# MLP products by one level of Strassen's algorithm, on one core

## The reference

```python
        x = x + merged @ w_out

        hm = _rmsnorm(x, g_mlp)
        x = x + jnp.square(jax.nn.relu(hm @ w_mlp_in)) @ w_mlp_out

    return _rmsnorm(x, g_final)
```

## Time and profile before

| | |
|---|---|
| time, median of 3 runs (lowest to highest) | 4360.57 us (4352.41 to 4361.17) |
| span of the profiled execution, first to last instruction | 4350.5 us |
| what the median has beyond that span | 10.1 us |
| TensorE busy in the span | 98% |
| the MLP stage in it | 3454.5 to 4350.5 us, 896 us |
| mean granted clock of TensorE | 0.994 |

### The profile page before, as it was taken

The page is one execution under the profiler, slowest core; times in us unless marked ns, Lnnn a source line. Parts: engine busy times, 40 slices in busy tenths (PEclk is TensorE's granted clock), DMA queues, the critical chain, the costliest instruction groups (busy, mean ns, idle before and its releaser), DMA issues. The chain is left out here.

```text
span 4350.5 us, 47027 instructions
## 1 busy us (share of the span) xinstructions
PE 4260.0 (98%) x18730; PEld 2510.2 (58%) x18730; DVE 1434.4 (33%) x3584; ACT 954.2 (22%) x1758; POOL 137.0 (3%) x215
## 2 busy tenths in 40 slices
PE   7999999999999999989999999999999999999999
PEld 4776666776556668567544565665544444444446
DVE  3246663664131255456255111112223300000003
ACT  4233332332123311154234111111111000000001
POOL 0000000000000000032010000010000000000000
PEclk9999999999999999999999999999999999999999
DMA  5310003112001111130121111122232011111111
GB/s 214 138 47 8 8 7 68 38 42 99 29 29 33 47 56 47 49 113 33 44 67 34 36 42 57 53 74 86 73 112 100 22 42 39 39 39 39 41 51 39
DMA packets 106458, 242.91 MB, mean 56 GB/s; under 512 B 15288, under 2 KB 47402, under 8 KB 105151
## 3 DMA queue, kind: packets, MB, share of 16 engines
q1 hardware_dynamic: 99264, 224.55, 16.0%
q0 software_dynamic: 5920, 13.25, 1.2%
q10 hardware_dynamic: 1056, 2.10, 0.1%
HBM read 202.80 MB, written 39.34 MB: 56 GB/s over the span
## 5 line engine op out<-in xcount | busy, mean ns | idle before, releaser
L2480 PE MATMUL upper_banks<-sbuf 128*128 128x512 f32 (+2 forms) x2112 | 812.2, 542 | 0.3 <-PEq L68 0.3
L345 PE MATMUL upper_banks<-sbuf 128*128 128x512 f32 x1792 | 769.8, 592 | 1.2 <-DVE sbuf L455 0.9
L2480 PEld LDWEIGHTS upper_banks<-sbuf 128*128 128x128 f32 x2112 | 392.7, 199 | 379.0 <-issue 373.7
L345 PEld LDWEIGHTS upper_banks<-sbuf 128*128 128x128 f32 x1792 | 340.2, 190 | 429.4 <-issue 427.1
L1894 PE MATMUL gla_prod<-sbuf 128*128 128x512 f32 (+1 forms) x784 | 319.7, 563 | 0.0
L1370 PE MATMUL mls_banks<-sbuf 128*128 128x512 f32 (+1 forms) x768 | 282.3, 522 | 2.0 <-PEq L68 1.5
L1894 PEld LDWEIGHTS gla_prod<-sbuf 128*128 128x128 f32 x784 | 147.5, 192 | 151.8 <-issue 143.8
L1370 PEld LDWEIGHTS mls_banks<-sbuf 128*128 128x128 f32 x768 | 143.1, 191 | 118.1 <-issue 110.8
L2726 ACT ACTIVATE sbuf<-upper_banks 128x512 f32<-128x512 f32 (+1 forms) x124 | 72.4, 584 | 618.3 <-PE upper_banks L2480 569.6
L860 PE MATMUL mla_banks<-sbuf 128*128 128x512 f32 (+1 forms) x416 | 176.0, 511 | 0.0
L423 ACT ACTIVATE sbuf<-upper_banks 128x1024 f32<-128x1024 f32 x32 | 32.8, 1024 | 622.5 <-PE upper_banks L345 622.5
(11 more groups left out here) (461 smaller groups left out, 5305.7 us busy)
## 6 DMA issues: line engine op xcount, KB each, us to landing
sbuf<-in_l_w_in SPq DMA_DIRECT2D x59, 512.0 KB, 3.8
sbuf<-in_w_in SPq DMA_DIRECT2D x52, 512.0 KB, 4.1
sbuf<-in_w_mlp_in SPq DMA_DIRECT2D x32, 512.0 KB, 3.6
sbuf<-in_w_mlp_out SPq DMA_DIRECT2D x32, 512.0 KB, 3.6
sbuf<-in_l_w_mod SPq DMA_DIRECT2D x24, 512.0 KB, 5.2
scratch_gates<-sbuf SPq DMA_DIRECT2D x48, 256.0 KB, 3.0
sbuf<-scratch_gates SPq DMA_DIRECT2D x8, 1536.0 KB, 6.6
sbuf<-in_l_w_mod SPq DMA_DIRECT2D x8, 1024.0 KB, 15.5
```

Source lines behind the costliest of these rows:

```text
L345: last = nc.tensor.matmul(prod[:, n % NB, o:o + 512], w[:, n % NB, k * P:(k + 1) * P], rhs, start=k == 0, stop=k == KD - 1)
L2480: last = nc.tensor.matmul(dst, lhsT, rhs, start=k == 0, stop=k == KD - 1)
```

## The change

The step pairs two output tiles, q and q+4, and takes both weight tiles at once (A, cut in 2 x 2 blocks: output tile q or q+4 by the first or last four k) against the activations (B, cut in 2 x 2: the first or last four feature rows by the first or second 512 tokens). In place of eight products of four matmuls, the step has seven, named P1 to P7, after Winograd's form of Strassen's algorithm:

- sums of weights, per step on GpSimd (line 374 on): S1 = A21 + A22, S2 = S1 - A11, S3 = A11 - A21 (in place of A21), S4 = A12 - S2, four instructions of 128 x 512;
- sums of activations on VectorE: T1 = B12 - B11, T3 = B22 - B12 (in place of B12), T2 = T3 + B11, and B21 - T2 for P4; once for `x` at the start (`xT`), once for each pair of hidden tiles (`twist_first`, `twist_last`, `hT`);
- sums of products: bank 0 of a step's three gathers P1, then P1+P6, then +P7, then +P4; bank 1 gathers P5, then P5+P3; bank 2 holds P2. Each state is read before the next product goes into the same bank.

In an up step ScalarE copies P1, P5 and P1+P6 to SBUF (`kept`), VectorE adds them to P5+P3, P1+P6+P7 and P2, and squares; in a down step VectorE alone adds each of the seven states to `acc`. There is one `hid` now, and the order is up f, down f. The last group's down steps run over two halves of 512 tokens, with products 256 wide, and load their weights once for each half; the final norm has two pieces of 512 in place of 512, 256 and 256. A step's two weight tiles are loaded when the step two before it has been multiplied.

```diff
-    steps = [("up", 0, j) for j in range(KD)]
-    for f in range(3):
-        steps += [("up", f + 1, j) for j in range(KD)]
-        steps += [("down", f, j) for j in range(KD)]
+    for f in range(4):
+        steps += [("up", f, q, 0) for q in range(4)]
+        steps += [("down", f, q, h) for h in range(2 if f == 3 else 1) for q in range(4)]
...
+    END = NS - 8
+    seq = [(0, "P1"), (0, "P2"), (1, "P1"), (1, "P2")]
+    seq += [(n, c) for c in ("P5", "P6", "P3", "P7", "P4") for n in (0, 1)]
+    seq += [(n, c) for n in range(2, NS) for c in ORDER]
...
+        def bank_of(n, c):
+            return bank(3 * (n % 2) + {"P1": 0, "P6": 0, "P7": 0, "P4": 0, "P5": 1, "P3": 1, "P2": 2}[c])
...
+            for n in range(2, NS):
+                kind, f, q, h = steps[n]
+                sp.wait_ge(mm, last_of[n - 2] + 1)
+                for i, j in enumerate((q, q + 4)):
...
+        @block.gpsimd
+        def _(pool):
...
+                nc.gpsimd.tensor_tensor(s1, a21, a22, ALU.add).then_inc(summed, 1)
+                pool.wait_ge(summed, 4 * n + 1)
+                nc.gpsimd.tensor_tensor(s2, s1, a11, ALU.subtract).then_inc(summed, 1)
+                nc.gpsimd.tensor_tensor(a21, a11, a21, ALU.subtract).then_inc(summed, 1)
+                pool.wait_ge(summed, 4 * n + 3)
+                nc.gpsimd.tensor_tensor(s4, a12, s2, ALU.subtract).then_inc(summed, 1)
...
+                if c == "P1":
+                    if n >= 2:
+                        for i in range(2):
+                            pe.wait_ge(w_ready[2 * (n % 2) + i], 16 * (n // 2))
+                        evicted(n - 2, "P4")
+                elif c == "P5":
+                    pe.wait_ge(summed, 4 * n + 1)
...
+                elif c == "P6":
+                    pe.wait_ge(summed, 4 * n + 3)
+                    evicted(n, "P1")
+                elif c == "P3":
+                    pe.wait_ge(summed, 4 * n + 4)
+                    evicted(n, "P5")
+                elif c == "P7":
+                    evicted(n, "P6")
+                else:
+                    evicted(n, "P7")
...
+                for k in range(4):
+                    if n == 0 and c in ("P5", "P6", "P4"):
+                        pe.wait_ge(xmade, {"P5": 1, "P6": 9, "P4": 13}[c] + k)
...
+                    last = nc.tensor.matmul(bank_of(n, c)[:, 0:wd], lw[:, k * P:(k + 1) * P], right_operand(c, base, tw, k, o, wd, to),
+                                            start=k == 0 and c in ("P1", "P5", "P2"), stop=k == 3, skip_group_check=True)
...
+            def down_event(n, c):
...
+                dve.drain()
+                dve.wait_ge(mm, at[(n, c)] + 1)
+                nc.vector.tensor_tensor(dst, bank_of(n, c)[:, 0:wd], dst, ALU.add).then_inc(dve_done, 1)
```

More of the change, by code:

```diff
@@ L312, in _ @@
             sp.dma_start(gf[:], io["g_final"]).then_inc(g_in, 16)
[L313 to L322, removed]
@@ L331, in _ @@
         @block.tensor
         def _(pe):
[L333 to L377, removed]
-                else:
[L379 to L392, removed]
-            def spread_out(p):
-                pe.wait_ge(rinvd, p + 1)
-                o, wd = PIECES[p]
-                spread(nc, factor(p), rcol, ident, range(o // P, (o + wd) // P)).then_inc(spreaded, 1)
@@ new lines, in sums_of, with spread_out @@
+            def sums_of(h):
+                pe.wait_ge(sq_add, 7 * (h + 1))
+                column_sums(nc, bank(7), total, ones, range(4 * h, 4 * h + 4)).then_inc(ssum, 1)
+            def spread_out(h):
+                pe.wait_ge(rinvd, h + 1)
+                spread(nc, bank(6 + h), rcol, ident, range(4 * h, 4 * h + 4)).then_inc(spreaded, 1)
+            pe.wait_ge(ahead, 64)
+            for i, (n, c) in enumerate(seq):
+                product(n, c)
+                if i == 0:
+                    pe.wait_ge(tail_sum, 1)
+                    column_sums(nc, bank(6)[:, 0:8], last_squares, ones, range(4)).then_inc(tail_ssum, 1)
+                if i == 1:
+                    pe.wait_ge(tail_inv, 1)
+                    spread(nc, bank(7), rcol, ident, range(4, 8)).then_inc(spreaded, 1)
+                if (n, c) == (END + 4, "P3"):
@@ new lines, in root @@
+            def root(h):
+                act.wait_ge(ssum, h + 1)
+                cols = slice(4 * h, 4 * h + 4)
+                nc.scalar.activation(rcol[:, cols], bank(7)[:, cols], ACT.Sqrt, bias=eps, scale=1.0 / D).then_inc(rooted, 1)
+            for e in range(16):
+                n, late = END + e // 2, e % 2
+                kind, f, q, h = steps[n]
+                act.wait_ge(dve_done, by_dve[(n, "P4" if late else "P2")])
+                if e == 0:
+                    nc.scalar.activation(rcol[:, 8:9], eps, ACT.Sqrt)
+                first = e % 8 == 0
+                if e >= 3:
+                    act.wait_ge(sq_add, e - 2 - (1 if e > 8 else 0))
+                nc.scalar.activation(total[:, 512 * h:512 * h + 512] if first else sq[:, e % 2, :],
+                                     acc[:, q + 4 * late, 512 * h:512 * h + 512], ACT.Square).then_inc(sqd, 1)
+                if e == 7:
@@ L504, in _, with normed @@
-            add_square(len(ends) - 1)
-            inverse(2)
-            for k in range(KD):
-                finish(2, k)
+            def normed(k):
+                nc.vector.scalar_tensor_tensor(out=x[:, k, 512:1024], in0=acc[:, k, 512:1024],
+                                               scalar=g[:, k:k + 1], in1=bank(7), op0=ALU.mult, op1=ALU.mult)
+            for k in range(4):
+                normed(k)
+            dve.drain()
+            for k in range(4):
+                nc.vector.tensor_tensor(xT[:, 0, k, :], x[:, k, 512:1024], x[:, k, 0:512], ALU.subtract).then_inc(xmade, 1)
@@ new lines, in _ @@
+            for k in range(4, 8):
+                normed(k)
+            dve.drain()
+            for k in range(4):
+                nc.vector.tensor_tensor(x[:, k, 512:1024], x[:, 4 + k, 512:1024], x[:, k, 512:1024], ALU.subtract).then_inc(xmade, 1)
+            dve.drain()
+            for k in range(4):
+                nc.vector.tensor_tensor(xT[:, 1, k, :], x[:, k, 512:1024], x[:, k, 0:512], ALU.add).then_inc(xmade, 1)
+            dve.drain()
+            for k in range(4):
+                nc.vector.tensor_tensor(xT[:, 2, k, :], x[:, 4 + k, 0:512], xT[:, 1, k, :], ALU.subtract).then_inc(xmade, 1)
```

278 lines of the change are left out of this document (175 added, 103 removed).

## The result

The changed kernel takes 4252.95 us (median of four runs, 4246.82 to 4256.75) where the kernel before takes 4360.62 (median of four, 4352.41 to 4361.17): a ratio of 0.9753, with a 95% interval of 0.9739 to 0.9768, or 107.7 us less. The prediction said 4252.0.

The account below looks back on a forecast made before the run. The prediction took TensorE's matmuls to bound the MLP stage. Its terms, -109.7 - 0.8 - 0.9 + 1.2 + 0.2 + 1.2 = -108.8 us, took the span from 4350.5 to 4241.7; with 10.1 added, the median was 4252 us, range 4245 to 4272.

Parts of the forecast that it names:

- TensorE is the bound: In the MLP stage, time is matmul count times time per matmul plus a tail; one product in eight less, -109.7 us.
- No bank is late: Banks are read before their next product, with 2.6 us to spare, 0.9 at the tightest place; no cost taken.
- Rival 1: A bubble at every change of product, 224 times 0.04 to 0.30 us: 4261 to 4319 us; chance 12%.
- Weight sums: GpSimd's sums at 1.2 us each, 128 of them, 150 us, ready before their products need them; no cost taken.
- Rival 2: GpSimd much slower than its row, S4 late in the last steps from 3.2 us a sum; 4301 at 4.7; chance 3%.
- Rival 3: Gaps at bank hand-overs lower TensorE's clock, making the kernel slower than before; 4444 us with a quarter affected; chance 3%.
- The start: At the stage's start, TensorE's wait for VectorE's first norm multiply is covered by products: -0.9 us.
- The load ahead of step 2: Step 2's weights are issued when step 0 ends, with only one product left to cover them: +1.2 us.
- The border to the last down steps: At group 3's hidden tiles, P1's fourth matmul waits for the last square, 1.5 us with 1.3 covered: +0.2 us.
- The tail: Behind the last product: 12.0 us in place of 10.8, +1.2 us; 1 to 2 us longer if stores lag.
- the 10.1 us: The kernel before's median lies this far above its profiled span; added to the forecast span to get the median.
- The shared port: VectorE instructions with two SBUF inputs and GpSimd's weight sums might exclude each other: about 1 to 3 us, 4255.

Follow-up runs that it names:

- eighth_back: Changed kernel with an eighth, unread product put back in steps 2 to 31: 4349.28 us, 0.9983 of the kernel before; MLP stage 886.9 us against 790.65.
- no_sums: Changed kernel without GpSimd's weight sums from step 2 on, the products using old sums: MLP stage 790.8 us against 790.65.
- sums_x3: Changed kernel with 12 weight sums a step on GpSimd in place of four, from step 4 on: MLP stage 821.5 us against 790.65.
- tile1_early: Changed kernel with each step's first weight tile loaded once P2 and the weight sums of two steps before are done: MLP stage 789.1 us against 790.65.
- p1_add_early: Changed kernel with VectorE adding P1 behind the first activation sum, not all four, at group 3's down steps: MLP stage 788.6 us against 790.65.
- three_edits: Changed kernel with P1's add earlier, first weight tile loaded early, two idle matmuls before the last sums: 0.9749 of the kernel before; stage 788.5 us against 789.7.

## Why the prediction was right, and where its sum was off

- **TensorE is the bound, and the time is its matmuls.** Right, and shown by eighth_back: 96.1 us of products put back made the stage 96.2 longer. The rates taken from the earlier trace rows held: 0.4293 us a record of 512 columns, 52.04 / 240 = 0.217 for 256.
- **No bank is late, and a change of product makes no bubble.** Right: in 1456 records, 182 products, not one wait. Rival 1 (9 to 67 us) did not happen. Its counter-evidence, the weight loads at 0.43 us through waits already met, was the right row.
- **Weight sums.** The duration was right (1.2 us taken, 1.27 measured), their number wrong: 36 steps give 144, not 128, and 183 us of work and not 150. That changed nothing, since no_sums shows a cost of zero. Rival 2, waits from 3.2 us a sum or 12.8 us for four, has its point bracketed: eight sums (11.2 us) waited once for 0.32 us, twelve (16.9) in seven of the eight narrow steps. The first waits were not at S4, which the prediction timed, but at S3 and, with twelve sums, at S1.
- **The clock.** Rival 3 did not happen: 1.00 in the middle of the products, with a change of bank every 3.43 us. The only work at a lower one is the last spread. That the mechanism is there is shown by sums_x3, where waits of 2.9 us and more brought the clock to 0.50; no wait of TensorE before the last product was that long in the changed kernel.
- **The start.** 0.9 us gained, as said: the chain has no wait there.
- **The load ahead of step 2.** +1.2 foretold, 5.11 - 3.43 = 1.67 us measured (3501.07 to 3506.18, of which P4's last matmuls cover 3.43; 1.4 to 1.7 in the other executions with these loads). The cause is shown by tile1_early. The pair was there 0.5 us later than the row of a pair from the middle of the stage had it.
- **The border to the last down steps** is the step that failed: +0.2 foretold, 1.5 us measured (4131.30 to 4188.26, 56.96 us, for 256 records that take 55.5). The part that the prediction followed, P1's wait for the last square, cost the 0.2 it said, as p1_add_early shows. It did not follow what VectorE has queued behind that square: four activation sums, and only then P1's add, for which P6 waits (a gap of 1.09 us). p1_add_early took 1.2 us of it away.
- **The tail.** 12.0 foretold, 13.5 measured (4231.50 to 4245.0). As far as the column sums it is 2.07 us, as said. From them to the first multiply it is 3.42 and not 2.2: eight records for 1.07 us, and the spread at a clock of 0.61, as the timeline of the changed kernel shows. The multiplies took 5.36 us, the stores kept up, and the end came 2.65 us behind the multiplies and not 2.4.

```profile
4232.04 1.48 DVE L586 TENSOR_TENSOR sbuf<-sbuf 128x512 f32<-128x512 f32 x2
4233.57 1.05 PE L109 MATMUL upper_banks<-sbuf 128*128 128x1 f32 x8 [2.08 <-DVE sbuf L586]
4235.19 1.76 PE L116 MATMUL upper_banks<-sbuf 128*128 128x128 f32 x8 [0.57 <-DVE sbuf L591]
4236.99 5.36 DVE L597 SCALAR_TENSOR_TENSOR sbuf<-sbuf,upper_banks 128x512 f32<-128x512 f32 x8 [1.85 <-PE upper_banks L116]
```

Together 0.5 + 1.3 + 1.5 = 3.3 us, and the span was 4245.0 for 4241.7. The median agreed to 1 us by luck: an execution's time is 1.8 us above its own span, and the rest of the 10.1 us that were added is the spread of runs, in which a median of four lands anywhere within 10 us. This time the median came 8.0 us above the profiled span, so 10.1 was 2.1 too much, and that hid 2.1 of the 3.3 that the span was short.

## The shared port

The prediction left it open whether VectorE and GpSimd hold each other up. They do. At the start of the changed kernel's stage (timeline):

```profile
3455.73 1.26 POOL L376 TENSOR_TENSOR sbuf<-sbuf 128x512 f32<-128x512 f32 x1
3455.78 1.76 DVE L494 TENSOR_TENSOR sbuf<-sbuf 128x512 f32<-128x512 f32 x1 [0.70 <-ACT sbuf L454]
3456.96 1.71 POOL L377 TENSOR_TENSOR sbuf<-sbuf 128x512 f32<-128x512 f32 x1
```

VectorE's add started 0.05 us behind a weight sum and ended 0.55 us behind that sum's end, in 1.76 us and not 0.69; the next weight sum took 1.71 and not 1.27. To 0.2 us that fits one waiting for the other's whole instruction, each in turn. In the changed kernel this cost TensorE nothing that shows (no_sums is as long), against the 1 to 3 us that the prediction set beside its sum, and the two seldom meet: its 64 squares have a mean of 693 ns, its weight sums one of 1266 to 1279. It shows as soon as they meet: with twice the sums, VectorE's adds of squares in the last 120 us have a mean of 980 ns in place of 692 (the group by line, count, busy and mean):

```profile
L590 DVE TENSOR_TENSOR sbuf<-sbuf 128x512 f32<-128x512 f32 x14 | 13.7, 980 | 1.3
```

and in three_edits one such meeting cost 0.77 us of the path. Which instructions are held is shown by the kernel with three times the sums, in which GpSimd works 65% of a wide stretch (590 as above, 557 the square, both with two inputs in SBUF; 550 the add of a product to a copy, with one input in PSUM):

```profile
L557 DVE SCALAR_TENSOR_TENSOR sbuf<-sbuf 128x512 f32<-128x512 f32 x57 | 58.0, 1018 | 14.6 <-ACT sbuf L466 10.0 <-issue 0.9
...
L590 DVE TENSOR_TENSOR sbuf<-sbuf 128x512 f32<-128x512 f32 x14 | 15.4, 1103 | 1.3
...
L550 DVE TENSOR_TENSOR sbuf<-upper_banks,sbuf 128x512 f32<-128x512 f32 x42 | 29.0, 691 | 205.3 <-PE upper_banks L427 205.3
```

The instructions with both inputs in SBUF take about one and a half times as long; the one with an input in PSUM keeps its 691 ns. The Trainium skill (SBUF — State Buffer, section "SBUF: two separate sides") states this exclusion for a VectorE instruction with two SBUF inputs against a GpSimd one that reads SBUF; the rows agree.

## What to carry to other kernels

Where one engine's products fill a stage without a gap, count its instructions and multiply by a rate from one long piece of the chain: work on the other engines costs nothing up to a point, and that point can be found by doubling it. Look for the losses at the borders, where the stream of a helping engine is crossed by one last result: write down what it has queued ahead of the instruction that frees a buffer, not only the instruction for which the next product waits. Look at the granted clock behind every wait of a few microseconds: in sums_x3 part of the price stood there and not in the waits. And take the length of the changed stage from the traces before comparing kernels that differ by less than their runs do.

## Not expected

- A program's runs differ by 10 us through stages that the change does not touch, while the MLP stage itself repeats within about 1 us.
- The same eight short matmuls at the end took 1.16 us at a clock of 1.00 in one execution and 1.76 at 0.61 in another, behind the same 2.08 us of idle time.
- Where GpSimd held TensorE up for 2.9 to 3.9 us, the granted clock was 0.50 for 2.5 to 6 us behind the wait; the mean of the narrow records is 407 ns in that kernel and 380 in the changed one.
